# Four rows of the gate and up weights to a partition, and two pieces in one transfer

## The reference, cut to what matters

```python
D_MODEL = D_FF = 1024; N_EXPERTS = 32; TOP_K = 4
logits = x2 @ w_router + b_router            # 288 tokens, 4 experts each
...
def expert_block(args):                      # xb: the tokens of one expert
    gu = xb @ w_gate_up[e] + b_gate_up[e]    # w_gate_up[e]: 1024 x 2048, 8 MB
    gt = jnp.minimum(gu[:, :D_FF], 7.0)
    up = jnp.clip(gu[:, D_FF:], -7.0, 7.0)
    glu = gt * jax.nn.sigmoid(gt * 1.702)
    return ((up + 1.0) * glu) @ w_down[e] + b_down[e]   # w_down[e]: 1024 x 1024, 4 MB
```

## Time and profile before

| What | Value |
|---|---|
| Median of 3 runs (lowest to highest) | 1272.7 us (1272.3 to 1273.05) |
| Span of the profiled execution, first to last instruction | 1270.4 us |
| PE busy in it | 1207.3 us, 95% |
| DVE, ACT, POOL busy | 414.9, 233.9, 74.2 us |
| Moved by DMA | 502.37 MB, mean 395 GB/s |
| Granted TensorE clock, mean | 0.997 |
| Chain that ended last | PE 64%, DMA 31% |
| Gate and up matmuls (line 1807, on `ring`) | 1232 of 596 ns, idle before them 22.0 us |
| Median us from issue to landing, g pieces to `ring` | 42.7 |

### The profile page before, as it was taken

The page is one execution under the profiler, slowest core; times in us unless marked ns, Lnnn a source line. Parts: engine busy times, 40 slices in busy tenths (PEclk is TensorE's granted clock), DMA queues, the critical chain, the costliest instruction groups (busy, mean ns, idle before and its releaser), DMA issues.

```text
span 1270.4 us, 14752 instructions
## 1 busy us (share of the span) xinstructions
PE 1207.3 (95%) x6107; PEld 512.1 (40%) x6122; DVE 414.9 (33%) x919; ACT 233.9 (18%) x459; POOL 74.2 (6%) x79
## 2 busy tenths in 40 slices
PE   9999999999999999999999999999998989999996
PEld 4456667675533333333333333333333333333332
DVE  3274653335532324223142222313131322222233
ACT  2212433230211111111121011111011110101012
POOL 0443004300200000000000000000000000000000
PEclk9999999999999999999999999999999999999998
DMA  9999999999799999999999999999999999999994
GB/s 339 392 309 365 343 370 316 292 316 421 265 400 387 429 428 427 428 429 427 428 428 426 428 429 427 427 427 428 428 428 429 428 427 428 428 428 429 428 427 177
DMA packets 74793, 502.37 MB, mean 395 GB/s; under 512 B 6993, under 2 KB 31185, under 8 KB 49105
## 3 DMA queue, kind: packets, MB, share of 16 engines
q1 hardware_dynamic: 72864, 497.10, 96.6%
q0 software_dynamic: 848, 2.36, 0.6%
q10 hardware_dynamic: 1008, 1.90, 0.4%
HBM read 498.42 MB, written 37.03 MB: 421 GB/s over the span
## 4 chain that ended last, share of the span: by engine, by line
PE 64%; DMA 31%; DVE 2%; issue 1%; SPq 1%; ACT 1%; DVEq 0%; ACTq 0%
PE ps L1807 20%; DMA ring<-in_w_gate_up 17%; PE ps L1846 10%; DMA tail<-in_w_gate_up 7%; DMA late<-in_w_gate_up 7%; PE ps L1276 6%; PE ps L1192 6%; PE ps L1763 3%; PE ps L1707 3%; PE ps L1557 2%; PE ps L1570 2%; PE ps L1824 1%; PE ps L1254 1%; PE ps L1322 1%; PE ps L1726 1%
## 5 line engine op out<-in xcount | busy, mean ns | idle before, releaser
L1807 PE MATMUL ps<-ring,cq 128*64 128x512 f32 x1232 | 280.4, 596 | 22.0 <-DMA ring<-in_w_gate_up 21.9
L1807 PEld LDWEIGHTS ps<-ring,cq 128*64 128x64 f32 x1232 | 84.0, 136 | 193.1 <-issue 144.2
L1846 PE MATMUL ps<-ring,cq 128*64 128x512 f32 x592 | 134.3, 595 | 0.7 <-issue 0.7
L1276 PE MATMUL ps<-arena,ring 128*128 128x288 f32 x384 | 102.6, 412 | 2.6 <-ACT ring L935 2.6
L1076 ACT ACTIVATE cq<-ps 128x512 f32<-128x512 f32 x32 | 19.1, 597 | 451.3 <-PE ps L1824 451.3
L2341 DVE TENSOR_REDUCE tail<-ps 128x1 f32<-128x288 f32 x15 | 6.9, 458 | 290.2 <-PE ps L1739 290.2
L1276 PEld LDWEIGHTS ps<-arena,ring 128*128 128x128 f32 x384 | 69.6, 189 | 26.5 <-issue 5.9
L1846 PEld LDWEIGHTS ps<-ring,cq 128*64 128x64 f32 x592 | 41.0, 136 | 73.3 <-issue 69.8
L2369 DVE TENSOR_TENSOR x_tok<-x_tok,ps 64x512 f32<-64x512 f32 (+2 forms) x51 | 43.9, 860 | 67.9 <-PE ps L1763 62.3
L1192 PE MATMUL ps<-ring,arena 128*128 128x512 f32 (+1 forms) x192 | 64.1, 597 | 0.4 <-DMA ring<-in_w_in 0.4
L1090 ACT ACTIVATE cq<-ps 64x512 f32<-64x512 f32 x32 | 18.9, 590 | 230.2 <-PE ps L1846 230.2
(11 more groups left out here) (390 smaller groups left out, 1313.6 us busy)
## 6 DMA issues: line engine op xcount, KB each, us to landing
ring<-in_w_gate_up SPq DMA_DIRECT2D x77, 2048.0 KB, 42.7
ring<-in_w_down SPq DMA_DIRECT2D x37, 2048.0 KB, 44.2
tail<-in_w_gate_up SPq DMA_DIRECT2D x13, 2048.0 KB, 41.0
late<-in_w_gate_up SPq DMA_DIRECT2D x12, 2048.0 KB, 42.0
cq<-in_w_gate_up SPq DMA_DIRECT2D x12, 2048.0 KB, 42.6
arena<-in_w_gate_up SPq DMA_DIRECT2D x12, 2048.0 KB, 43.3
ring<-in_w_in SPq DMA_DIRECT2D x9, 2048.0 KB, 12.4
out_dil_k_s<-in_cache_dil_k SPq DMA_DIRECT2D x8, 2044.0 KB
```

The source lines that it names most:

```text
L1276: ins = pe.matmul(bank(gate_bank(m))[:, 0:TT], wblk[AREA[6 + m // 4]][:, k, (m % 4) * P:(m % 4 + 1) * P], hT_v[:, k, :], start=(k == 0), s ...
L1807: ins = pe.matmul(bank(gu0 + u)[64 * h:64 * h + 64, :], xTe[:, k % 4, (k // 4) * 64:(k // 4) * 64 + 64], pair_buf[slot][:, a:a + 512], sta ...
L1846: ins = pe.matmul(bank(7 if last else 5)[64 * h:64 * h + 64, :], aT[:, kk % 4, (kk // 4) * 64:(kk // 4) * 64 + 64], pair_buf[slot][:, a:a ...
```

## The change

Every g piece is now dealt with four rows to a partition. The 1024 rows of an expert's gate and up weights are taken as two blocks of 512; partition p has rows 4p to 4p + 3 of a block, 32 KB that lie together in HBM, and a piece is one half of that. Where an even g piece and the next one fall on slots (4,5), (6,7) or (8,9), which are now neighbours in `ring`, one transfer of 4 MB with 32 KB to a partition brings both (`load_wide`). SP issues it when the second of the two slots is free, and TensorE waits for the one semaphore before either piece. Slots (0,1) and (2,3) are not neighbours, so the g pieces on them stay single, as do all d pieces and pieces 0 to 11. `arena` changes from slot 9 to slot 3, and the order of the first ten loads is now 0, 1, 2, 5, 4, 6, 7, 8, 3, 9, with the same waits at the same places. The tokens' transposes pick every fourth column, and the gain follows. SP reads the number of overflow blocks three pieces later.

```diff
-        gain_rows[2].reshape(4, P, 2).transpose(1, 0, 2).reshape(P, KC)], 1), dtype=np.float32)
+        gain_rows[2].reshape(2, P, 4).transpose(1, 0, 2).reshape(P, KC)], 1), dtype=np.float32)
...
+        pair_buf = [late[:, 0:2 * SLOT], cq[:, NINTH:NINTH + 2 * SLOT], tail[:, 0:2 * SLOT],
+                    arena[:, MASKS:MASKS + 2 * SLOT]] + [ring[:, 2 * SLOT * i:2 * SLOT * (i + 1)] for i in (0, 1, 4, 5, 2, 3)]
+        wide_buf = {4: ring[:, 0:4 * SLOT], 6: ring[:, 8 * SLOT:12 * SLOT], 8: ring[:, 4 * SLOT:8 * SLOT]}
...
+        def is_wide(i):
+            return i >= NSLOT + HALVES and i % NSLOT in wide_buf and stream[i][0] == "g"
+        landed, count = [], [0] * NSLOT
+        for i in range(len(stream)):
+            if i and is_wide(i - 1):
+                landed.append(landed[-1])
+                continue
+            count[i % NSLOT] += 16
+            landed.append((i % NSLOT, count[i % NSLOT]))
+        def up_rows(rows, k):
+            return rows[512 * (k // 2):512 * (k // 2) + 512].rearrange("(p c) n -> p (c n)", c=4)[:, 2 * SLOT * (k % 2):2 * SLOT * (k % 2 + 1)]
...
-                    src = d["w_gate_up"][0, e, 256 * k:256 * (k + 1), :].rearrange("(p c) n -> p (c n)", c=2)
+                    src = up_rows(d["w_gate_up"][0, e], k)
...
+            def load_wide(i):
+                _, e, k = stream[i]
+                src = d["w_gate_up"][0, e, 256 * k:256 * k + 512, :].rearrange("(p c) n -> p (c n)", c=4)
+                sp.dma_start(wide_buf[i % NSLOT], src).then_inc(pair_in[i % NSLOT], 16)
...
-            for i in W_BR:
-                wait_wblk_used(sp, i)
-                load_pair(i - 9)
+            wait_wblk_used(sp, 12)
+            load_pair(5)
+            wait_wblk_used(sp, 13)
+            load_pair(4)
             sp.wait_ge(S["merged"], 8)
-            load_pair(5)
             load_pair(6)
-            for n in range(2):
-                sp.wait_ge(S["wout_done"], 5 + n)
-                load_pair(7 + n)
+            load_pair(7)
+            sp.wait_ge(S["wout_done"], 5)
+            load_pair(8)
+            sp.wait_ge(S["wout_done"], 6)
+            load_pair(3)
             load_pair(9)
...
-                wait_pair_used(i - NSLOT)
-                load_pair(i)
-                if stream[i] == ("g", COUNT_AT, 3):
+                if is_wide(i - 1):
+                    continue
+                if is_wide(i):
+                    wait_pair_used(i + 1 - NSLOT)
+                    load_wide(i)
+                else:
+                    wait_pair_used(i - NSLOT)
+                    load_pair(i)
+                if stream[i] == ("g", COUNT_AT + 1, 0):
...
-                ins = act_e.activation(xg_sb[:, 256 * half:256 * half + 256], bank(6)[:, 256 * half:256 * half + 256], ACT.Copy)
+                ins = act_e.activation(xg_sb.rearrange("p (f c) -> p f c", c=4)[:, :, 2 * half:2 * half + 2],
+                                       bank(6).rearrange("p (f c) -> p f c", c=4)[:, :, 2 * half:2 * half + 2], ACT.Copy)
...
-                    rows = xg_sb[:, 256 * (q // 2):256 * (q // 2) + 256].rearrange("p (f c) -> p c f", c=2)[:, q % 2, :]
+                    rows = xg_sb.rearrange("p (f c) -> p c f", c=4)[:, q, :]
...
-                    slot, landed = pair_at("g", b, k // 2)
+                    slot, told, landed = pair_at("g", b, k // 2)
...
-                        pe.wait_ge(pair_in[slot], landed)
+                        pe.wait_ge(pair_in[told], landed)
```

More of the change, by code:

```diff
@@ L151, in build @@
         NINTH = 3816
+        HALVES = 2
         kT = late[:, 2304:2304 + 3 * TT]
@@ L443, in build @@
         r_cmp = area(early, 0, NOV, NE)
-        pair_buf = [late[:, 0:2 * SLOT], cq[:, NINTH:NINTH + 2 * SLOT], tail[:, 0:2 * SLOT]] + [ring[:, 2 * SLOT * i:2 * SLOT * (i + 1)] for i in (1, 0, 4, 5, 2, 3)] + \
-            [arena[:, MASKS:MASKS + 2 * SLOT]]
+        pair_buf = [late[:, 0:2 * SLOT], cq[:, NINTH:NINTH + 2 * SLOT], tail[:, 0:2 * SLOT],
+                    arena[:, MASKS:MASKS + 2 * SLOT]] + [ring[:, 2 * SLOT * i:2 * SLOT * (i + 1)] for i in (0, 1, 4, 5, 2, 3)]
+        wide_buf = {4: ring[:, 0:4 * SLOT], 6: ring[:, 8 * SLOT:12 * SLOT], 8: ring[:, 4 * SLOT:8 * SLOT]}
         g_final = pair_buf[6][:, 0:D]
@@ L459, in pair_at @@
                 i = place[(kind, b, k)]
-                return i % NSLOT, 16 * (i // NSLOT + 1)
+                return i % NSLOT, *landed[i]
             i = k if kind == "g" else 4 + k
-            fixed = len(range(i, len(stream), NSLOT))
-            return i, 16 * (b + (fixed - NE + 1))
+            return i, i, 16 * (b + (count[i] // 16 - NE + 1))
         KV_OUT = 16 * 10
         NPAIR = NE // 2
-        HALVES = 2
         COUNT_AT = 8
@@ L728, in load_dyn @@
                 if kind == "g":
-                    src = d["w_gate_up"][0][bass.ds(e, 1), 256 * k:256 * (k + 1), :].rearrange("o (p c) n -> (o p) (c n)", c=2)
+                    src = d["w_gate_up"][0][bass.ds(e, 1), 512 * (k // 2):512 * (k // 2) + 512, :] \
+                        .rearrange("o (p c) n -> (o p) (c n)", c=4)[:, 2 * SLOT * (k % 2):2 * SLOT * (k % 2 + 1)]
                 else:
                     src = d["w_down"][0][bass.ds(e, 1), 512 * k:512 * (k + 1), :].rearrange("o (p c) n -> (o p) (c n)", c=4)
-                i, _ = pair_at(kind, b, k)
+                i, _, _ = pair_at(kind, b, k)
                 return sp.dma_start(pair_buf[i], src).then_inc(pair_in[i], 16)
@@ L1835, in down @@
                 for j in range(j0, j1):
-                    slot, landed = pair_at("d", b, j // 2)
+                    slot, told, landed = pair_at("d", b, j // 2)
                     if j % 2 == 0:
```

## The result

The changed kernel takes 1278.18 us (median of 10 runs, 1277.15 to 1282.86) against 1272.88 us before (1271.77 to 1276.72, 10 runs). The ratio is 1.0039, 95% interval 1.0028 to 1.0049: 5.0 us more, 3.6 to 6.2. The forecast was 6.9 us more: inside its own stated bounds, but above the measured interval. The profiled span is 1276.1 us, 5.7 over that of before.

A forecast was written before the change was run, and what follows sets the result against it. The DMA was taken to bound the stream, and piece 186's landing the end. End wait 4.9 plus early gap 3.0 minus rate 1.0 gave 6.9 us more, 1272.7 to 1279.6; likeliest case's range 1277.7 to 1281.1, wider range 1273 to 1284.

The forecast's parts named there:

- What bounds the kernel: Whole stream: TensorE eats a stock of ten pieces until 712 us, DMA sets the time, piece 186's landing holds the end.
- The early gap: Near 385 us: wide transfers of pieces 16 to 19, issued late, let the DMA run dry; 3.0 us lost, 2.3 to 3.5.
- The end: Expert 31: piece 186 is usable only when 187 has landed, 4.9 us later.
- the pieces 184 and 185 would not bind: Expert 31: both land 9.8 us before 187, and k = 0 to 3 end by 1233.8, before 1234.1.
- The rate: Stream: 36 wide transfers with 32 KB packets save 1.0 us, bounds 0 and 2.2.
- the straight line: Packet cost fitted from 2 KB and 16 KB packets: 62 ns saved a wide transfer, 2.2 us for 36.
- The 72 us: Gain for 36 transfers if each paid the skill's 2.0 us fixed cost; the forecast said the trace does not agree.
- A: Rival, stream: 32 KB packets raise the rate by more than the waits cost, needing 2.2%; faster; chance 0.08.
- D: Rival, stream: larger packets are slower by 1%, 3.5 us more than with no gain, 1284.1; chance 0.07.
- E: Rival, wide transfers: 32 KB runs are cut into 16 KB packets, no rate gain, 1280.6; counted with the likeliest case.
- B: Rival, no difference: early gap only 1.5 us and rate gains 4.0, 1275.1; chance 0.17, two thirds within the bound.
- C: Rival, TensorE: longer waits lower its granted clock, adding some 4 us in the last expert, 1283.6; chance 0.08.

The follow-up runs named there:

- Kernel 1: Changed kernel with no wide transfers, every piece alone in 2 MB; new dealing, slot order and strided copies kept: 1272.70 us, ratio 0.9999 against the kernel before.
- kernel 2: Changed kernel, but pieces 16 to 19 come alone and the other 34 wide transfers stay: 1275.35 us, ratio 1.0019 against the kernel before.
- kernel 9: Changed kernel, but all pieces alone, each issued when its own slot is free; TensorE still waits for both landings: 1276.93 us, ratio 1.0033.
- kernel 11: Changed kernel, but only pieces 16 with 17 and 18 with 19 are wide: 1276.23 us, ratio 1.0026 against the kernel before.
- kernel 12: Changed kernel, but only pieces 184 with 185 and 186 with 187 are wide: 1277.48 us, ratio 1.0038 against the kernel before.
- kernel 3: Changed kernel, but expert 31's pieces 184 to 187 come alone and the other 34 wide transfers stay: 1274.27 us, ratio 1.0013 against the kernel before.
- kernel 4: Changed kernel, but pieces 16 to 19 and 184 to 187 come alone; 32 wide transfers stay: 1272.25 us, ratio 0.9998 against the kernel before.
- kernel 6: Changed kernel plus three extra matmuls before each TensorE wait for a wide transfer from expert 12 on: 1283.38 us, ratio 1.0074 against the kernel before.
- kernel 10: Changed kernel plus three extra matmuls only before TensorE's first wait of expert 31: 1278.11 us, ratio 1.0048 against the kernel before.
- Kernel 5: Changed kernel with wide transfers only from piece 24 to 149, 26 of them: 1271.71 us, ratio 0.9980 against the kernel before.
- kernel 8: Changed kernel, but each wide transfer issued as two of 2 MB with 16 KB packets at the same moment; TensorE waits for both: 1280.76 us, ratio 1.0059.
- kernel 7: Kernel 4 plus four extra matmuls before TensorE's wait for piece 174: 1271.08 us, ratio 0.9986 against the kernel before.

## Why the prediction was right, and where a size was off

**What bounds the kernel.** The stock, the DMA-bound stream, and an end held by the landing of piece 186: right. Kernel 1 gives the time before. Kernels 2, 9, 11 and 12, in which A or the last wait was changed, moved by about what was changed; kernels 3 and 4 moved by less, for a reason that the forecast does not have (see below).

**The early gap.** Forecast 3.0 us (2.3 to 3.5), from 12.7 to 14.6 us to landing for 4 MB in an empty queue; measured 13.5 and 13.7 us, A 3.4 us longer. Kernels 2 and 11 show it alone: by the ratios 2.5 us given back, 3.3 us lost.

**The end.** Forecast 4.9 us, which kernels 9 and 12 bear out. That the pieces 184 and 185 would not bind came out right only by luck, by 0.04 us where the forecast had 0.3 to spare. Its 9.5 us for k = 0 to 3 was not made for a falling clock, and with it they took 9.6 (1223.40 to 1233.02); in kernel 12, where the clock fell for longer, TensorE was the later of the two. Kernel 12 shows the cost alone (4.8 by the ratio), kernel 9 the late use without the late issue and without the packets (4.2 by the ratio).

**The rate: the term that was mis-sized.** Forecast 1.0 us saved, within 0 to 2.2. B is 827.1 us in the mean of the five kernels without a wide transfer in it (826.3 to 827.4) and 824.9 in the mean of the seven that have 26 to 34 of them, 32 in the mean (823.9 to 825.8; kernel 6, with its extra matmuls, is not among them, and its 823.7 fits): 2.2 / 32 = 0.07 us each, 2.5 for 36. In the forecast I let the nearest row, the halves with 8 KB packets, halve the value of the straight line from 2 KB to 16 KB packets; the line's 62 ns was the better guide. The changed kernel's own B is another microsecond shorter, which is no more than B's scatter between like kernels. With 3.4 for the gap and 2.5 for the rate the forecast's sum is 4.9 + 3.4 - 2.5 = 5.8 us, within the measured 3.6 to 6.2; the forecast's 6.9 is 1.9 above the measured 5.0: the rate's term accounts for 1.5, the gap's 0.4 goes the other way, and 0.8 is left, which the interval covers. The fit of 2.0 us and the bytes that the forecast takes from the Trainium skill's "DMA: Bandwidth & Descriptors" stands there in the section "Anatomy of one DMA — SWDGE (gpsimd) path", not under Bandwidth, and for transfers that GpSimd issues; here SP issues them. Its rules (section "Rules for kernel authors") ask for 1 MiB or more to a DMA, which the 2 MB pieces have already. The 72 us worked out from the fit were not there: the gain was 0.07 us a transfer and not 2.0.

**The rivals.** A: the rate rose, by under 1%, far from the 2.2% that it would have needed; 0.07 us a transfer where 0.22 were needed. Single slices of 32 us reach 434 and 435 GB/s, over the 433 that the forecast named as a sign of being wrong, but from 450 to 1150 us the mean is 428.9 against 427.8 before. D and E are out: no slower, and the trace has 4608 packets of 32 KB, 128 for each of the 36 transfers. B is out by kernels 2 and 11 (its sum took 4.0 us from the rate, beyond the forecast's own bound of 2.2, and two thirds of its 0.17 are 0.11, not 0.13). C was given 0.08, and its mechanism was there: the clock fell 0.4 us behind the wait before expert 31, as the window above shows. Its price at the end was zero, since TensorE was due to wait for a landing right afterwards (kernel 10); what the six falls before it cost no run here tells (kernel 6 does not), but each is followed by waits for landings. Forecast waits of up to 4 us were right; that they are long enough for the clock, I had put as unlikely. The Trainium skill's "TensorE: Matmul & The Clock Gate" (section "HAM oscillation — how this bites in real kernels") says that waits for DMA in a matmul loop can send the engine back to the lower clock again and again; the trace agrees, with seven stretches at 0.50, one of them in the window shown.

**What I had not seen.** Taking the two costs away does not leave the gain (kernel 4). A wide transfer near the end also makes TensorE late for what follows, some 5 us, and where nothing is waited for afterwards the fallen clock costs in full. The slack is about 2.3 us an expert, and not the 2.6 of kernel 5's expectation. This is my estimate from kernel 4: two experts of the stream are 12 pieces of 4.89 us, 58.7 us, and TensorE's own work for two is 1227.49 - 1172.04 - 1.3 = 54.1. Two experts of slack, 4.6 us, do not make up for 4.9 and 1.3. Kernel 5, with none in the last six experts and none in the first 400 us, beats both the kernel before and the changed one: 2.5 us under the kernel before by ratio (1.4 to 3.8).

## What to carry to other kernels

Merging transfers in a queue that is already full gains little, here 0.07 us in 9.8, the cost of the packets, since the 2.9 us that a lone piece takes over its bytes are hidden there; it costs wherever the queue is short (the start) and wherever the last bytes are waited for (the end), for the merged transfer is issued when its last slot is free and used when its last byte has landed. So merge in the middle of a stream and keep small pieces at both ends. When two costs are removed and the gain does not show, read what holds the end now: here it had passed from the DMA to TensorE.

## What the runs showed of the hardware

- The granted clock fell to 0.50 (1.2 GHz) after waits of TensorE of 2.3 us (kernel 1, 848 to 851 us), 2.2 us (kernel 4, from 1172.5 us) and 2.6 us (the changed kernel, from 1223.8 us), each between long busy stretches; the 8, 16 or 32 matmuls behind took 1.3 to 1.7 us longer. It is not every such wait: behind one of 2.54 us at 791 us, in the changed kernel, 32 matmuls took 7.09 us, and behind another of 2.54 us at 1087 us they took 8.78. The length alone does not settle it: it stayed at 1.00 behind one of 3.09 us (the changed kernel, 880 us) and fell behind one of 1.86 us (kernel 7, 1131 us).

TensorE's timeline of kernel 1 and its window there, then two waits of the changed kernel:

```profile
847.83 5.34 PE L1839 MATMUL ps<-ring,cq 128*64 128x512 f32 x16 [2.32 <-DMA ring<-in_w_gate_up]
```

```profile
848.00:851.00 3.00, 3.00 (x8) 0.84 (x10) 0.00 (x0) 0.00 (x0) 0.00 (x0) 0.50 1.00 426
```

```profile
791.13 7.09 PE L1839 MATMUL ps<-ring,cq 128*64 128x512 f32 x32 [2.54 <-DMA ring<-in_w_gate_up]
...
1086.55 8.78 PE L1839 MATMUL ps<-ring,cq 128*64 128x512 f32 x32 [2.54 <-DMA ring<-in_w_gate_up]
```

- Packets of 32 KB moved at about 432 GB/s (4.19 MB between landings 9.7 us apart), packets of 16 KB at 428; one took 1217.6 ns in the mean, the other 615.6 (the changed kernel and kernel 8, 450 to 1150 us). Runs of 16 KB at a pitch of 32 KB in HBM were as fast as adjacent ones (B 827.3 in kernel 1 and before).
- A transfer of 4 MB issued into an empty or nearly empty queue landed after 13.4 to 14.2 us, one of 2 MB alone after 7.8; behind a full queue it adds 9.7 and 4.9.
